# A gap of 288 bytes per partition in front of three large SBUF buffers

## The chip, the cores and the metric

The kernel runs on one core of a Trainium2 chip. The metric is the device time of one execution, in microseconds (us). Smaller is better.

## The reference, cut to what matters

The reference runs two small models one after the other on 256 tokens of width 1024: a block with multi-head latent attention, an mLSTM mixer and two squared-ReLU MLPs, then a block with a short convolution, a sparse attention with shared keys and values, and four SwiGLU feed-forward layers. Nearly all of its arithmetic is products of the token matrix with weights:

```python
D_MODEL = 1024; SEQ = 256; D_FF = 4 * D_MODEL; D_FF_2 = 2816

def sqrelu_mlp(h, w1, w2):
    return jnp.square(jax.nn.relu(h @ w1)) @ w2

def swiglu_ffn(x, w_in, w_out):
    gate, up = jnp.split(x @ w_in, 2, axis=-1)
    return (jax.nn.silu(gate) * up) @ w_out
...
y = mla_mixer(hn, ...)        # layer 0: projections 1024 to 384, 256, 32, back to 1024
y = mlstm_mixer(hn, ...)      # layer 1: projections 1024 to 3072, 8, back to 1024
x = x + y.astype(x.dtype)
x = x + sqrelu_mlp(rms_norm(x, norm_ffn[i]), ffn_w1[i], ffn_w2[i]).astype(x.dtype)
```

All of it is in float32, and each weight is used for all 256 tokens once.

## The kernel before, in words

**Split products.** A float32 product is made from three products in the type fp32r: a weight w is split into w_hi and w_lo, and a feature x into x_hi and x_lo, and w_hi·x_hi + w_hi·x_lo + w_lo·x_hi is added up in PSUM. All weights come from DRAM as a stream of 522 tiles `raw` of 128 partitions by 1024 floats (4096 bytes per partition). Each tile goes through a ring of four slots: SyncE issues the load, ScalarE makes `w_hi` from `raw` (line 510), VectorE makes `w_lo` as raw minus w_hi (line 968; GpSimd does 46 of the 522, line 448), and TensorE consumes it. Semaphores `tile_loaded`, `hi_ready`, `lo_ready` and `tile_done` tie the four together. A tile holds eight blocks of 128x128 weights, each 512 bytes per partition.

**The three forms of product.** TensorE's program (from line 1638 on) has:
- `product` (lines 1643 and 1644, in `residual`): a weight load of a w_hi block and one matmul of 512 columns, x_hi and x_lo together, out of `hs`; then a weight load of the w_lo block and a matmul of 256 columns, x_hi. It is used by down_0, down_1 and out_0 to out_3.
- `narrow_product` (lines 1651, 1652 and 1653, in `feature` and `residual_one`): three weight loads (w_hi, w_hi, w_lo), each with a matmul of 256 columns out of `xs`, `os` or `hs`. It is used by up_0, up_1, glu_0 to glu_3, cin and all the smaller projections.
- `token_major` (lines 1779 to 1781): the roles are turned. Blocks of 128 columns of `xs` or `os` are loaded as the weights, and the matmul streams 512 columns out of w_hi or w_lo. It is used by uk, uq, uv, mv, mo, kv and nq.

The attention's own products and its transposes (lines 1804 to 2034) are plain float32, with operands in `arena`, `kT`, `vtok` and `con`.

**The memory.** The helper `sb` allocates a tensor that stays for the whole kernel, one behind the other. First come raw, w_hi and w_lo (twelve buffers of 4096 bytes per partition), x, then many small ones, the last of them `vtok`, `kcT` and `vc`. Behind these lie three large regions. Two of them have two names each, since a tensor that is allocated and left at once gives its address to the next:

```python
        with nc.sbuf_tensor("os", [P, KD * 2 * S], F32R) as os_:
            pass
        bias = sb("bias", [P, H * S])
        with nc.sbuf_tensor("w1c_all", [P, 2 * 16 * P], F32) as w1c_all:
            pass
        xs = sb("xs", [P, KD * 2 * S], F32R)
        with nc.sbuf_tensor("hs", [P, FF1 * 2 * S], F32R) as hs:
            pass
        arena = sb("arena", [P, FF1 * 2 * S])
```

So `os` and `bias` are one region of 16,384 bytes, `w1c_all` and `xs` another of 16,384, and `hs` and `arena` a third of 65,536. Each chunk of x_hi or x_lo in `xs`, `os` and `hs` is 256 floats, 1024 bytes. All weight blocks begin at the same place modulo 512 bytes, and so do all chunks of xs, os and hs. Between the two places there are 32 bytes before the change: a chunk begins 32 bytes past a block modulo 512.

**The order of the work.** TensorE goes through the stages in the order of the network. Around the edited lines there are only allocations, no instruction. `bias` is filled once, by eight transfers that ScalarE issues before the sparse attention (line 939), when `os` is no longer in use.

```python
            def product(out_bank, lhs, k, src, first, last, hi=0):
                s, c = lhs
                chunk = k * 2 * S
                pe.matmul(bank(out_bank), w_hi[s][:, c:c + P], src[:, chunk:chunk + 2 * S], start=first, stop=False)
                return pe.matmul(bank(out_bank, 0, S), w_lo[s][:, c:c + P], src[:, chunk:chunk + S], start=False, stop=last)
...
                out = bank(out_bank, 0, S)
                pe.matmul(out, w_hi[s][:, c:c + P], x_hi, start=first, stop=False)
                pe.matmul(out, w_hi[s][:, c:c + P], x_lo, start=False, stop=False)
                return pe.matmul(out, w_lo[s][:, c:c + P], x_hi, start=False, stop=last)
```

Of the kernel before, what the change touches and what calls it, by code (L numbers as in the profile page):

```python
# [30 lines left out]
P = 128  # L31
# [105 lines left out]
def build(nc, x_in, tiles, vecs, rows, consts, rel_bias, w1c_k, w1c_v, w2c_k, w2c_v, y_out):  # L137
    ctx = ExitStack()
    with ctx:
        def sb(name, shape, dt=F32):  # L140
            return ctx.enter_context(nc.sbuf_tensor(name, shape, dt))
# [30 lines left out]
        kcT = sb("kcT", [P, G * NC])  # L172
        vc = sb("vc", [G * NC, G * DH])

        with nc.sbuf_tensor("os", [P, KD * 2 * S], F32R) as os_:
            pass
        bias = sb("bias", [P, H * S])
# [2031 lines left out]
```

## Time and profile before

| what | value |
|---|---|
| median of 3 runs | 1664.65 us (1664.22 to 1665.67) |
| the profiled execution's own time | 1666.71 us |
| its span, first to last instruction | 1664.9 us |
| mean granted clock of TensorE | 0.985 of full speed |
| TensorE matmul busy | 1602.7 us, 96% of the span |
| VectorE busy | 1099.6 us, 66% |
| ScalarE busy | 885.4 us, 53% |
| DMA | 282.81 MB, mean 170 GB/s |

A matmul's record begins when it starts and ends when its last result is modelled to be out, so records of successive matmuls overlap. The pace of TensorE is read from start to start, or from the number of matmuls in a stretch in which it never rests, and not from the duration of one.

### The profile page before, as it was taken

How to read it: one execution, taken by the hardware profiler on the slowest of the kernel's cores; microseconds unless marked ns; L12 is line 12 of the kernel's file. 1: busy time of each engine (PE TensorE's matmuls, PEld its weight loads, DVE VectorE, ACT ScalarE, POOL GpSimd, SP SyncE). 2: the span in 40 equal slices, each digit the busy share in tenths (PEclk: the TensorE clock that was granted, in tenths of full speed). 3: DMA queues.
4: the chain of work that ended last, by engine and by line, in shares of the span. 5: the costliest groups of instructions: out<-in, count | busy, mean ns of one | idle time of the engine just before them, and what ended most of it. 6: DMA issues, size and time to landing. Idle time of an engine off the chain costs nothing.

```text
span 1664.9 us, 33598 instructions
## 1 busy us (share of the span) xinstructions
PE 1602.7 (96%) x11652; PEld 1510.1 (91%) x11652; DVE 1099.6 (66%) x1770; ACT 885.4 (53%) x1468; POOL 163.7 (10%) x141
## 2 busy tenths in 40 slices
PE   7899999999999999999999999997999988799999
PEld 7789998977999899998999999897999867799997
DVE  6667766544876667667877666785566728676665
ACT  5676554535655445455446445544545546664443
POOL 1640000266000000000000000000000053300000
PEclk9999999989999999999999999998999989999999
DMA  6136566544566556556655555656455680055564
GB/s 228 64 82 199 188 190 190 176 131 135 178 190 188 191 176 198 182 187 203 191 188 189 190 188 187 206 182 196 145 189 186 210 171 15 1 175 186 184 197 142
DMA packets 81246, 282.81 MB, mean 170 GB/s; under 512 B 8848, under 2 KB 12432, under 8 KB 81168
## 3 DMA queue, kind: packets, MB, share of 16 engines
q1 hardware_dynamic: 77376, 276.88, 52.4%
q10 hardware_dynamic: 3792, 4.85, 1.7%
q8 instruction: 54, 0.88, 0.2%
q14 instruction: 24, 0.20, 0.0%
HBM read 280.12 MB, written 1.57 MB: 169 GB/s over the span
## 4 chain that ended last, share of the span: by engine, by line
PE 88%; DVE 5%; ACT 3%; issue 2%; DMA 1%; ACTq 1%; POOL 0%; DVEq 0%; SPq 0%; POOLq 0%
PE psum L1651 17%; PE psum L1653 17%; PE psum L1652 17%; PE psum L1643 17%; PE psum L1644 9%; PE psum L1779 2%; PE psum L1780 2%; PE psum L1781 2%; ACT arena L853 1%; DMA raw<-tiles 1%; DVE w_lo L968 1%; PE psum L2034 1%; PE psum L1941 1%; DVE arena L1517 0%; DVE arena L1516 0%
## 5 line engine op out<-in xcount | busy, mean ns | idle before, releaser
L510 ACT ACTIVATE w_hi<-raw 128x1024 fp32r<-128x1024 f32 x522 | 550.5, 1056 | 462.8 <-PE psum L1653 266.3
L968 DVE TENSOR_TENSOR w_lo<-raw,w_hi 128x1024 fp32r<-128x1024 f32 x476 | 582.0, 1223 | 229.0 <-ACT w_hi L510 228.2
L1651 PE MATMUL psum<-xs,w_hi 128*128 128x256 f32 x1960 | 550.7, 281 | 6.1 <-DVE w_lo L968 5.0
L1653 PE MATMUL psum<-xs,w_lo 128*128 128x256 f32 x1960 | 549.8, 280 | 0.0
L1652 PE MATMUL psum<-xs,w_hi 128*128 128x256 f32 x1960 | 547.9, 280 | 0.0
L1643 PE MATMUL psum<-hs,w_hi 128*128 128x512 f32 x1216 | 421.9, 390 | 0.0
L1651 PEld LDWEIGHTS psum<-xs,w_hi 128*128 128x128 f32 x1960 | 369.6, 189 | 7.2 <-DVE w_lo L968 5.5
L1652 PEld LDWEIGHTS psum<-xs,w_hi 128*128 128x128 f32 x1960 | 369.7, 189 | 0.2
L1653 PEld LDWEIGHTS psum<-xs,w_lo 128*128 128x128 f32 x1960 | 369.2, 188 | 0.0
L1644 PE MATMUL psum<-hs,w_lo 128*128 128x256 f32 x1216 | 343.4, 282 | 0.0
L1643 PEld LDWEIGHTS psum<-hs,w_hi 128*128 128x128 f32 x1216 | 228.3, 188 | 47.1
L448 POOL TENSOR_TENSOR w_lo<-raw,w_hi 128x1024 fp32r<-128x1024 f32 x46 | 110.3, 2411 | 1228.1 <-ACT w_hi L510 1198.0
L1644 PEld LDWEIGHTS psum<-hs,w_lo 128*128 128x128 f32 x1216 | 230.5, 190 | 0.0
L1651 PE MATMUL psum<-os,w_hi 128*128 128x256 f32 x544 | 154.5, 284 | 1.6 <-DVE os L1158 1.6
L1652 PE MATMUL psum<-os,w_hi 128*128 128x256 f32 x544 | 152.7, 281 | 0.0
L1653 PE MATMUL psum<-os,w_lo 128*128 128x256 f32 x544 | 152.6, 281 | 0.0
L1651 PEld LDWEIGHTS psum<-os,w_hi 128*128 128x128 f32 x544 | 103.2, 190 | 2.5 <-DVE os L1158 2.4
L1652 PEld LDWEIGHTS psum<-os,w_hi 128*128 128x128 f32 x544 | 103.2, 190 | 0.0
L1653 PEld LDWEIGHTS psum<-os,w_lo 128*128 128x128 f32 x544 | 103.1, 189 | 0.0
L991 DVE SCALAR_TENSOR_TENSOR xs<-x,vec,xs 128x256 fp32r<-128x256 f32 (+1 forms) x80 | 38.1, 482 | 51.7 <-ACT xs L524 51.7
L524 ACT ACTIVATE xs<-x,vec (+1 forms) x80 | 40.2, 509 | 54.3 <-DVE x L1058 31.2
L1106 DVE TENSOR_TENSOR fsum<-psum,sil 128x256 f32<-128x256 f32 x88 | 37.4, 425 | 46.0 <-PE psum L1653 44.7
(282 smaller groups left out, 1643.8 us busy)
## 6 DMA issues: line engine op xcount, KB each, us to landing
raw<-tiles SPq DMA_DIRECT2D x522, 512.0 KB, 4.2
bias<-bias_dram ACTq DMA_DIRECT2D x8, 256.0 KB, 12.5
x<-x_in SPq DMA_DIRECT2D x4, 256.0 KB, 5.7
y_out<-x SPq DMA_DIRECT2D x8, 128.0 KB, 3.5
con<-consts SPq DMA_DIRECT2D x1, 771.0 KB, 9.2
bias_dram<-bias_row ACTq DMA_DIRECT2D x1, 512.0 KB, 7.2
row<-rows SPq DMA_DIRECT2D x1, 192.0 KB, 9.2
vec<-vecs SPq DMA_DIRECT2D x1, 80.5 KB, 1.9
```

The lines of the kernel that those rows point to most:

```text
L448: pool.tensor_tensor(w_lo[s][:, :], raw[s][:, :], w_hi[s][:, :].bitcast(F32), ALU.subtract).then_inc(lo_ready, 1)
L510: act.activation(w_hi[s][:, :], raw[s][:, :], ACT.Copy).then_inc(hi_ready, 1)
L524: act.activation(dst, src, ACT.Copy, scale=gain).then_inc(xhi_ready, 1)
L968: dve.tensor_tensor(w_lo[s][:, :], raw[s][:, :], hi_of(w_hi[s][:, :]), ALU.subtract).then_inc(lo_ready, 1)
L991: dve.scalar_tensor_tensor(out=dst, in0=src, scalar=gain, in1=hi_of(hi), op0=ALU.mult, op1=ALU.subtract).then_inc(xs_ready, 1)
L1106: dve.tensor_tensor(f, bank(b, 0, S), sil[u // 2][:, :] if u % 2 else rb[:, :], ALU.mult).then_inc(out_read, 1)
L1643: pe.matmul(bank(out_bank), w_hi[s][:, c:c + P], src[:, chunk:chunk + 2 * S], start=first, stop=False)
L1644: return pe.matmul(bank(out_bank, 0, S), w_lo[s][:, c:c + P], src[:, chunk:chunk + S], start=False, stop=last)
L1651: pe.matmul(out, w_hi[s][:, c:c + P], x_hi, start=first, stop=False)
L1652: pe.matmul(out, w_hi[s][:, c:c + P], x_lo, start=False, stop=False)
L1653: return pe.matmul(out, w_lo[s][:, c:c + P], x_hi, start=False, stop=last)
L1779: pe.matmul(out, x_hi, w_hi[s][:, col:col + 512], start=c == 0, stop=False)
```

## The change

One allocation is added, of 72 floats (288 bytes) per partition, that nothing reads or writes. The three large regions behind it move up by 288 bytes, and so begin 320 bytes past the weight blocks modulo 512, where they began 32 past them. No instruction is added, removed or moved.

```diff
--- before.py
+++ after.py
@@ -172,6 +172,7 @@
         kcT = sb("kcT", [P, G * NC])
         vc = sb("vc", [G * NC, G * DH])
 
+        sb("apart", [P, 72])
         with nc.sbuf_tensor("os", [P, KD * 2 * S], F32R) as os_:
             pass
         bias = sb("bias", [P, H * S])
```

## Rows read from the trace of the kernel before

**Rows 1.** The page: its head, and the busy time of each engine.
```profile
span 1664.9 us, 33598 instructions
...
PE 1602.7 (96%) x11652; PEld 1510.1 (91%) x11652; DVE 1099.6 (66%) x1770; ACT 885.4 (53%) x1468; POOL 163.7 (10%) x141
```

**Rows 2.** The page: the chain that ended last, by engine and by line.
```profile
PE 88%; DVE 5%; ACT 3%; issue 2%; DMA 1%; ACTq 1%; POOL 0%; DVEq 0%; SPq 0%; POOLq 0%
PE psum L1651 17%; PE psum L1653 17%; PE psum L1652 17%; PE psum L1643 17%; PE psum L1644 9%; PE psum L1779 2%; PE psum L1780 2%; PE psum L1781 2%; ACT arena L853 1%; DMA raw<-tiles 1%; DVE w_lo L968 1%; PE psum L2034 1%; PE psum L1941 1%; DVE arena L1517 0%; DVE arena L1516 0%
```

**Rows 3.** Groups of instructions, shapes apart: xcount, busy us, mean ns, idle before.
```profile
L1651 PE MATMUL psum<-xs,w_hi 128*128 128x256 f32 x1960 | 550.7, 281 | 6.1 <-DVE w_lo L968 5.0 <-DVE xs L991 1.1
L1643 PE MATMUL psum<-hs,w_hi 128*128 128x512 f32 x1216 | 421.9, 390 | 0.0
L1644 PE MATMUL psum<-hs,w_lo 128*128 128x256 f32 x1216 | 343.4, 282 | 0.0
L1651 PE MATMUL psum<-os,w_hi 128*128 128x256 f32 x544 | 154.5, 284 | 1.6 <-DVE os L1158 1.6
L1779 PE MATMUL psum<-w_hi,xs 128*128 128x512 f32 x128 | 55.3, 432 | 0.2 <-DVE w_lo L968 0.2
L1779 PE MATMUL psum<-w_hi,os 128*128 128x512 f32 x34 | 14.3, 419 | 2.3 <-issue 2.3
L1651 PE MATMUL psum<-hs,w_hi 128*128 128x256 f32 x64 | 17.9, 280 | 0.0
```

**Rows 4.** Stretches: busy us and instructions per engine, clock, DMA share, GB/s.
```profile
420.00:520.00 100.00, 100.00 (x858) 99.95 (x857) 76.17 (x120) 62.25 (x112) 0.00 (x0) 1.00 0.61 186
640.00:720.00 80.00, 80.00 (x681) 80.00 (x681) 51.78 (x71) 38.25 (x56) 0.00 (x0) 1.00 0.59 188
```

**Rows 5.** Timeline of TensorE in down_0 (product): start us, duration us.
```profile
259.81 0.39 PE L1643 MATMUL psum<-hs,w_hi 128*128 128x512 f32 x1
260.04 0.28 PE L1644 MATMUL psum<-hs,w_lo 128*128 128x256 f32 x1
260.16 0.39 PE L1643 MATMUL psum<-hs,w_hi 128*128 128x512 f32 x1
...
262.12 0.28 PE L1644 MATMUL psum<-hs,w_lo 128*128 128x256 f32 x1
262.24 0.39 PE L1643 MATMUL psum<-hs,w_hi 128*128 128x512 f32 x1
```

**Rows 6.** Timeline of TensorE in mo (token_major): first and last of 40 starts.
```profile
372.36 0.40 PE L1781 MATMUL psum<-w_hi,xs 128*128 128x512 f32 x1
...
381.46 0.40 PE L1781 MATMUL psum<-w_hi,xs 128*128 128x512 f32 x1
```

**Rows 7.** Timeline of TensorE in the sparse attention, plain float32; x2 merges two.
```profile
1400.60 0.60 PE L2006 MATMUL psum<-kT,arena 128*128 128x256 f32 x2
1401.03 0.39 PE L2005 MATMUL psum<-kT,arena 128*128 128x128 f32 x2
1401.25 0.60 PE L2006 MATMUL psum<-kT,arena 128*128 128x256 f32 x2
1401.68 1.50 PE L2034 MATMUL psum<-vtok,arena 128*128 128x128 f32 x12
```

**Rows 8.** Groups on VectorE and ScalarE, moved buffers beside unmoved ones.
```profile
L1080 DVE TENSOR_TENSOR hs<-fsum,hs 128x256 f32 x144 | 60.4, 419 | 0.0
L1068 DVE TENSOR_TENSOR ssq<-ssq,sq 128x256 f32<-128x256 f32 x40 | 16.8, 420 | 0.0
L596 ACT ACTIVATE hs<-fsum 128x256 f32 x80 | 32.1, 401 | 1.1 <-DVE fsum L1106 1.1
L562 ACT ACTIVATE sq<-x 128x256 f32 x40 | 16.0, 401 | 0.0
```

**Rows 9.** The page, transfers: KB each, median us from issue to landing.
```profile
raw<-tiles SPq DMA_DIRECT2D x522, 512.0 KB, 4.2
bias<-bias_dram ACTq DMA_DIRECT2D x8, 256.0 KB, 12.5
```

**Rows 10.** Timeline of ScalarE's queue, and the chain that ended last: start us, us, what.
```profile
1331.38 0.35 ACTq L939 DMA_DIRECT2D bias<-bias_dram  x1
...
1342.19 12.90 DMA raw<-tiles
```

## The prediction

> **What bounds the kernel now.** I read the page first. TensorE is busy for 96% of the span and its weight loads for 91%, while VectorE stands at 66% and ScalarE at 53% [rows 1]. The chain that ended last confirms it: 88% of it is TensorE, and the eight lines of the three split products hold about 83 points of that [rows 2]. The groups by line tell how many matmuls that is, and that TensorE waited in front of the 1960 matmuls of line 1651 on xs for 6.1 us in all [rows 3]. So the time is the number of matmuls times the pace at which TensorE takes them, and the pace is the one thing that a shift of addresses could touch.
>
> The pace has to be read from start to start. In the stretch 420 to 520 us (narrow_product out of os, then xs) TensorE never rests at full clock and starts 858 matmuls in 100 us: **116.6 ns** each. In 640 to 720, the same code with xs in another layer, it is 80 us / 681 = 117.5 ns [rows 4]. In product, the starts of line 1643 at 259.81 and 262.24 us are seven pairs apart: 2.43 us / 7 = **347 ns** a pair; from each start of 1643 to that of 1644 it is 0.23 us (260.04 − 259.81), rounded to 10 ns, and the pair less a 256-column matmul of 117 gives 230 [rows 5]. In token_major, 39 intervals lie between 372.36 and 381.46 us: 9.10 / 39 = **233.3 ns** for 512 columns [rows 6].
>
> **What those paces hold that is not arithmetic.** At the level of 2.4 GHz, 256 columns at one a cycle are 106.7 ns and 512 are 213.3. The plain float32 products show how near TensorE comes to such a number with a weight load in front of each: two matmuls of 256 columns of line 2006 go from 1401.25 to 1401.68 us, 215 ns each, and the two of 128 columns of line 2005 from 1401.03 to 1401.25, 110 ns each [rows 7]. That is two cycles a column (213.3 and 106.7) and 2 to 3 ns on top. The split products have the same numbers of cycles and 10 ns (256 columns), 17 ns (the 512 of product) and 20 ns (the 512 of token_major) on top. So 7 to 18 ns per matmul are lost in the split products that are not lost in the plain ones. What takes them the trace does not name. It is not a fixed length: 512 columns cost 230 ns in product and 233.3 in token_major, with one weight load each. What differs there is which operand lies where: in product the stream begins 32 bytes past the weights modulo 512, in token_major it is the weights that lie 32 past the stream.
>
> **The change, part by part.** *Added instructions: none. Removed: none. Order: none.* The allocation is not written or read, so nothing waits for it. What it does is move os/bias, xs/w1c_all and hs/arena.
>
> *VectorE and ScalarE on the moved buffers: zero.* A 128x256 operation of VectorE takes 419 ns where it writes hs and 420 where it touches only unmoved buffers; on ScalarE it is 401 and 401 [rows 8]. If an address did cost them something, both have room: 76% and 62% busy in the densest stretch [rows 4].
>
> *Transfers: zero, between −2 and +2 us.* The 522 tiles go to raw, which does not move. The moved bias is filled by eight transfers of 12.5 us each, issued from 1331.38 us on [rows 9, 10], and here the DMA is not hidden: the chain waits 12.90 us for the tiles behind them, from 1342.19 on [rows 10]. The bytes stay the same, and no row shows that the place of a row modulo 512 costs a transfer anything; if it changed a sixth of that wait, it would be 2 us, which no side of the argument needs.
>
> *TensorE's plain products: zero to −0.5 us.* They are at 110 and 215 ns, and nothing can be won but the 2 to 3 ns.
>
> *TensorE's split products: the whole question.* There are 3 × (1960 + 544 + 64) = 7704 matmuls of narrow_product, 1216 pairs of product, and 3 × (128 + 34) = 486 matmuls of token_major [rows 3]. That makes 7704 + 2432 + 486 = 10,622 weight loads, each running beside a stream. No row shows a fp32r product at another offset than ±32, so the price is bounded. **Lower bound of the time:** every matmul falls to the pace of the plain ones: 7704 × (116.6 − 109) = 58.6, 1216 × (347 − 215 − 109) = 28.0, 486 × (233.3 − 215) = 8.9, in all −95.5 us. **Upper bound:** the nearest row for what an offset can do is the difference between 230 and 233.3, and read directly between starts (0.23) it is at most 5; I take 4.5 ns per load as the size of such an effect: 10,622 × 4.5 = +48 us. **What I take:** −4.5 ns per load, −48 us, which is also half of the lower bound. The reason for the sign: at 32 bytes' distance the two streams, which both move at 4 bytes a column through the same 512 residues, run close to each other; 320 sets them more than half a period apart. With the roles turned and the distance the other way the loss is larger, so the distance seems to matter, and the near one is the suspect. The loss also isn't a constant of the code: the same three lines go at 116.6 and at 117.5 ns in two layers [rows 4], as two streams would that fall into step in more than one way.
>
> The sum, for the profiled execution: 1666.71 − 48 = 1618.7 us. The median of the runs stands 2.06 us below that execution, so the forecast is 1664.65 − 48 = **1617 us**.
>
> *Is the next engine in the way?* In narrow_product a weight tile lasts 24 × 116.6 = 2.80 us; at 109 it would be 2.62. VectorE is busy 76.17 us in 100 there, 2.13 us per tile, ScalarE 1.74. A tile lands 4.2 us after issue [rows 9] and the ring holds four, 10.5 us at the faster pace. The DMA engines would rise from 0.61 to 0.65 busy [rows 4]. So nothing takes the gain back in the steady stages, and the stages in which TensorE waits for attention keep their time.
>
> **A rule against it.** TensorE's weight loads and streams do overlap here, and the loss beside them is 10 ns for 256 columns [rows 4]. The Trainium skill, TensorE: Matmul & The Clock Gate, section Step-by-step: what each phase is for, says that TensorE reads SBUF by two independent ports, one for the stream and one for LDWEIGHTS, so that loading weights takes no bandwidth from the running matmul; SBUF — State Buffer, section SBUF: two separate sides, adds that on the engines' side only the port pair shared by VectorE and GpSimd is contended. By that rule no address can matter and the time stays at 1664.65 us. The trace neither confirms nor refutes it: the plain products keep to it and the split ones lose something.
>
> **Rivals.**
> 1. *No change.* The 10 to 20 ns on top are the price of fp32r loads and streams as such, whatever their addresses; the 3 ns between product and token_major come from what stands before each matmul (a 256-column one in one, a 512-column one in the other). For it: plain products with operands at several offsets all keep their 110 and 215. Time: 1664.65, within 3 us. Chance 0.27.
> 2. *All of the loss goes.* 1664.65 − 95.5 = 1569. For it: the plain products prove that the pace can be had with a load per matmul. Against: the fp32r stream takes twice the bytes per cycle. Chance 0.10.
> 3. *Slower.* The streams pass each other at another point. If a load runs a fixed time behind the stream, or reads its columns in the other order, 320 can be the near distance and 32 the far one; then each load costs the 4.5 ns more: 1664.65 + 48 = 1712. It decides as soon as the pace of narrow_product is above 116.6; at the second level that the trace has, 117.5, it is 0.9 × 10,622 = +10 us, 1674. For it: the trace has no row at 320, and 32 may be good by luck. Chance 0.18.
> 4. *The gap does not do what it says*, because the allocator rounds or places it elsewhere. 288 is nine times 32, and all buffers behind it are allocated in order, so I see no way; what there is of it is in rival 1.
>
> **How the numbers follow.** The forecast, a partial gain of 15 to 75 us, has 0.45; its own range is 1590 to 1650. Together with rival 2, faster has 0.55, same (within 0.2%, 3.3 us, which is about what a measurement of this kernel can tell) 0.27, slower 0.18. The range has to take in the forecast, rival 1, most of the way to the floor and the small form of rival 3: 1580 to 1676. It leaves out about 0.07 below and 0.12 above.
>
> **What would show it.** Right: the stretch 420 to 520 us of the changed kernel holds over 870 matmuls (115 ns; 891 would be 112.2) with the same weight loads, the pairs of product come at less than 343 ns, token_major at less than 232, line 2006 stays at 215, and VectorE's 419 and 420 stay. The busy shares of VectorE and ScalarE rise slightly, as the same work lies in less time. Rival 1: 858 and 347 again. Rival 3: under 850. Wrong as a whole: the time moves though these paces don't, that is, by waits in attention or by the wait of 12.90 us behind the transfers of bias.

## The result, and the profile after

Over five runs the changed kernel takes 1674.46 us (1670.84 to 1676.04) where the kernel before takes 1665.67 us (1664.22 to 1666.79) beside it. The ratio is 1.0049, with a 95% interval of 1.0035 to 1.0064: **slower by half a per cent**. The profiled execution took 1674.46 us, with a span of 1672.7.

The page of the kernel after, its head and the busy time of each engine, against [rows 1]:

```profile
span 1672.7 us, 33598 instructions
...
PE 1613.2 (96%) x11652; PEld 1513.7 (90%) x11652; DVE 1100.1 (66%) x1770; ACT 885.8 (53%) x1468; POOL 163.9 (10%) x141
```

The same 33,598 instructions, and the same work on VectorE and ScalarE to within 0.5 us. Only TensorE is busy longer, by 10.5 us. All line numbers are one higher than before, because of the added line. The groups by line show which of TensorE's forms changed, against [rows 3] and [rows 8]:

```profile
L1644 PE MATMUL psum<-hs,w_hi 128*128 128x512 f32 x1216 | 427.2, 394 | 0.0
...
L1081 DVE TENSOR_TENSOR hs<-fsum,hs 128x256 f32 x144 | 60.4, 419 | 0.0
L597 ACT ACTIVATE hs<-fsum 128x256 f32 x80 | 32.2, 402 | 1.1 <-DVE fsum L1107 1.1
```

One 512-column matmul out of hs now shows 394 ns where it was 390. The means of narrow_product and of product's second matmul move by 3 ns at most, and downward. The durations say little, though; the pace says it. Stretches of the kernel after, TensorE alone (busy us and instructions, clock, DMA share, GB/s):

```profile
240.00:300.00 60.00, 60.00 (x341) 1.00 0.59 182
540.00:600.00 60.00, 60.00 (x346) 1.00 0.59 189
640.00:720.00 80.00, 80.00 (x681) 1.00 0.56 187
1210.00:1260.00 50.00, 50.00 (x444) 1.00 0.58 193
1490.00:1590.00 100.00, 100.00 (x851) 1.00 0.58 189
```

and the same stretches of the kernel before:

```profile
240.00:300.00 60.00, 60.00 (x348) 1.00 0.63 191
540.00:600.00 60.00, 60.00 (x348) 1.00 0.58 183
1210.00:1260.00 50.00, 50.00 (x431) 1.00 0.57 188
1490.00:1590.00 100.00, 100.00 (x859) 1.00 0.61 194
```

TensorE is never idle in any of them and its granted clock is 1.00, so the counts are paces. In down_0 (240 to 300 us) 341 matmuls instead of 348. In down_1 (540 to 600) 346 instead of 348, though it is the same code and the same buffer. In glu_3 (1490 to 1590) 851 instead of 859. In glu_0 (640 to 720) 681 in both [rows 4]. And in glu_2 (1210 to 1260) **444 instead of 431**: 112.6 ns a matmul, faster than anything in the trace before. The pairs of product in the kernel after:

```profile
259.72 0.40 PE L1644 MATMUL psum<-hs,w_hi 128*128 128x512 f32 x1
...
262.20 0.40 PE L1644 MATMUL psum<-hs,w_hi 128*128 128x512 f32 x1
...
539.67 0.39 PE L1644 MATMUL psum<-hs,w_hi 128*128 128x512 f32 x1
...
542.11 0.39 PE L1644 MATMUL psum<-hs,w_hi 128*128 128x512 f32 x1
```

Seven pairs each: 2.48 us / 7 = 354 ns in down_0 and 2.44 / 7 = 349 ns in down_1, where before it was 347 [rows 5]. The stretch that the prediction names for its test, up_1 with what stands before it, lies 5 us later in the kernel after:

```profile
425.00:525.00 100.00, 100.00 (x850) 1.00 0.56 184
```

That is 850 matmuls instead of 858. In token_major 40 intervals between 377.20 and 386.53 us are 233.3 ns each, as before. So the shift does change the pace of the split products. It changes it in steps, not everywhere alike, and mostly for the worse.

### The profile page after: what moved, and what is told of

Its sections match the earlier page's. It is cut to its first block, busy times and chain, and to the rows that moved or that the text cites. A ratio compares the mean times of both kernels' runs of the same rounds, so it can differ in the third digit from the quotient of the medians.

```text
span 1672.7 us, 33598 instructions
## 1 busy us (share of the span) xinstructions
PE 1613.2 (96%) x11652; PEld 1513.7 (90%) x11652; DVE 1100.1 (66%) x1770; ACT 885.8 (53%) x1468; POOL 163.9 (10%) x141
## 4 chain that ended last, share of the span: by engine, by line
PE 88%; DVE 5%; ACT 3%; issue 2%; DMA 1%; ACTq 1%; POOL 0%; DVEq 0%; SPq 0%; POOLq 0%
PE psum L1652 17%; PE psum L1654 17%; PE psum L1653 17%; PE psum L1644 17%; PE psum L1645 9%; PE psum L1780 2%; PE psum L1781 2%; PE psum L1782 2%; ACT arena L854 1%; DMA raw<-tiles 1%; DVE w_lo L969 1%; PE psum L2035 1%; PE psum L1942 0%; DVE arena L1518 0%; DVE arena L1517 0%
## 5 line engine op out<-in xcount | busy, mean ns | idle before, releaser
L511 ACT ACTIVATE w_hi<-raw 128x1024 fp32r<-128x1024 f32 x522 | 550.2, 1056 | 463.7 <-PE psum L1654 265.0
L969 DVE TENSOR_TENSOR w_lo<-raw,w_hi 128x1024 fp32r<-128x1024 f32 x476 | 582.1, 1223 | 229.8 <-ACT w_hi L511 228.9
L1644 PE MATMUL psum<-hs,w_hi 128*128 128x512 f32 x1216 | 427.2, 394 | 0.0
```

The costliest lines, as they stand in the source:

```text
L511: act.activation(w_hi[s][:, :], raw[s][:, :], ACT.Copy).then_inc(hi_ready, 1)
L969: dve.tensor_tensor(w_lo[s][:, :], raw[s][:, :], hi_of(w_hi[s][:, :]), ALU.subtract).then_inc(lo_ready, 1)
```

## The experiments

These theories stood at first. **A**: the distance between stream and weights sets the pace. **Its rivals**: the distance does not matter and something else in the kernel changed (B below), ScalarE and VectorE reading and writing beside TensorE set the paces (C), the absolute place of the streams counts, or only the mere presence of the gap. From part 4 on there is **A2**, a finer A: a distance allows several paces, and what ran just before a stage picks one. What is called distance below is how far the stream begins past its weights, in bytes.

**1. The products alone, at sixteen distances** (`e1_offsets_alone`). The core of the kernel, for each distance, with `m` in the place of xs and `w` in that of w_hi and w_lo:

```python
pe.matmul(bank(t % 4, 0, S), w[(t + (j == 2)) % 4][:, k * P:(k + 1) * P], m[:, 8 + k * 512 + (j == 1) * S:][:, 0:S], start=k == 0 and j == 0, stop=k == 7 and j == 2)
```

> This kernel computes nothing of the reference: it only runs the three forms of split product on filled buffers, at sixteen offsets of the streamed buffer against the weights (0 to 480 bytes in steps of 32), first with the other engines idle and then with ScalarE and VectorE copying 128x1024 tiles all the time. Theory A, the distance modulo 512 sets the pace: at 32 narrow_product goes at 116.6 ns and product at 347 ns a pair, at 320 at 117.7 and 351, and other offsets differ from both by ns. Theory B, the distance does not matter and the 351 came from something else in the kernel: all sixteen agree within 0.5 ns. Theory C, the paces come from ScalarE and VectorE reading and writing beside TensorE: the two passes differ.

The timeline of TensorE merges each group, so a pace is the step from one start to the next, divided by the number of matmuls. The rows are those of the distances 32, 64, 192 and 256, first narrow_product (x144), then product (x64, 32 pairs), and for 32 and 192 token_major (x48):

```profile
55.56 16.96 PE L91 MATMUL psum<-m,w 128*128 128x256 f32 x144
72.36 11.27 PE L95 MATMUL psum<-m,w 128*128 128x512 f32 x64
83.46 11.36 PE L98 MATMUL psum<-w,m 128*128 128x512 f32 x48
94.66 17.13 PE L102 MATMUL psum<-m,w 128*128 128x256 f32 x144
111.62 11.33 PE L106 MATMUL psum<-m,w 128*128 128x512 f32 x64
...
252.74 16.49 PE L146 MATMUL psum<-m,w 128*128 128x256 f32 x144
269.07 11.46 PE L150 MATMUL psum<-m,w 128*128 128x512 f32 x64
280.37 11.15 PE L153 MATMUL psum<-w,m 128*128 128x512 f32 x48
...
330.88 17.44 PE L168 MATMUL psum<-m,w 128*128 128x256 f32 x144
348.15 11.47 PE L172 MATMUL psum<-m,w 128*128 128x512 f32 x64
```

At 32, narrow_product goes at (72.36 − 55.56) / 144 = 116.7 ns and product at 11.10 / 32 = 346.9 ns a pair. At 64 narrow_product has 117.8, at 192 it has 113.4, and product 11.30 / 32 = 353.1. At 256 narrow_product has 119.9. All sixteen distances of the same trace, by their starts:

| distance | narrow_product, ns | product, ns a pair | token_major, ns |
|---|---|---|---|
| 32 and 288 | 116.7 | 347.0 | 233.3 |
| 64 and 320 | 117.8 | 348.8 | 233.4 |
| 96 and 352 | 119.9 | 350.3 | 234.0 |
| 128 and 384 | 120.0 | 350.9 | 232.2 |
| 160 and 416 | 118.7 | 347.0 | 233.2 |
| 192 and 448 | 113.4 | 353.1 | 228.9 |
| 224 and 480 | 118.3 | 352.8 | 233.2 |
| 256, and 0 in the second pass | 119.9 | 353.4 | 226.9 |

Three things follow. Theory A holds for the products by themselves, though the distance 320 gives 348.8 a pair and not the 351 that was expected. **The period is 256 bytes and not 512**: each pair of rows 256 apart agrees within 0.6 ns, so the change went from 32 to 64, the next step of 32, and not to the far side. And the second pass, with ScalarE and VectorE each busy 97% of the time, gave the same paces (narrow_product at 32, 116.7 again, at 192, 113.4 again), so theory C falls. GpSimd and the DMA queues rest in this run, so it says nothing of them.

**2. A gap of 512, a gap of 256, a gap in front of everything, a gap of 224** (`e2_gap512`, `e8_gap256`, `e3_front288`, `e4_gap224`). The edits are one line each:

```diff
-        sb("apart", [P, 72])
+        sb("apart", [P, 128])    # or 64, or 56; for e3 the 72 floats stand in front of raw
```

> A gap of 512 bytes instead of 288: the large buffers lie 32 bytes past the weights modulo 512 again, as before, at other addresses. Theory A (distance modulo 512): the time of before, 1665 us within 3 us, pairs of product at 347 ns. Rival (the absolute place, or the mere shift, or the build, costs something): 1670 to 1676 us as with the change.

> The gap of 288 bytes in front of all buffers: everything moves by 288, the distance between weights and streams stays 32. Theory A: 1665 us, pairs at 347 ns. Rival (the absolute address of the streams modulo 512 counts, not the distance): 1670 to 1676 us, pairs at 351 ns, as with the change.

> A gap of 224 bytes: the large buffers lie 256 past the weights modulo 512. Theory A: another time than at 32 and at 320, somewhere between 1655 and 1690 us, with the pace of the pairs that the offset 256 shows in the kernel with the products alone. Rival (only a whole multiple of 512 against anything else counts): 1670 to 1676 us like the change.

> A gap of 256 bytes, the large regions 288 past the weights. Period 256: the time of before, 1665 us within 3 us, pairs at 346.9 ns. Period 512: another time, as for the change (1672 us) or the gap of 224 (1694 us).

Measured, as ratios to the kernel before: gap 512, 1.0004 (0.999 to 1.0018); 288 in front of everything, 1.0000 (0.9988 to 1.0013); gap 256, 0.9996 (0.9985 to 1.0007); gap 224, **1.0175** (1.0153 to 1.0198), 1694.3 us. The gap as such costs nothing, moving everything together by 288 costs nothing, and the distances 32, 288 and 544 are one. The distance 256, which is 0 modulo the true period, is the slowest tried in the whole kernel, and 4 us outside the 1655 to 1690 that were expected for it. Its stretches in glu_0 and glu_3:

```profile
640.00:720.00 80.00, 80.00 (x669) 1.00 0.59 191
...
1490.00:1590.00 100.00, 100.00 (x834) 1.00 0.58 188
```

80 / 669 = 119.6 and 100 / 834 = 119.9 ns, as the products alone showed at 256.

**3. The weights moved instead of the stream, finer steps, and plain float32** (`e5_offsets_fine`).

> Again only products on filled buffers, nothing of the reference: distances 0 to 248 bytes in steps of 8, then pairs with the weights moved instead of the stream, then plain float32 products at distances 0 to 224. Theory A, the distance between stream and weights modulo 256 sets the pace: stream +32 with weights +32 gives what distance 0 gave (120 ns for narrow_product), weights +32 with the stream at 0 gives what 224 gave (118.3 ns), weights +32 and stream +64 what 32 gave (116.7), weights +64 and stream at 0 what 192 gave (113.4). Rival, the place of the stream alone counts: each pair gives what its stream's own place gave. Plain float32: no dependence, within 1 ns, as its stream takes half the bytes per cycle; the rival that any product depends on it would show some ns here too.

The timeline again. The groups are stream +32 with weights +32 (L416, L420), stream +224 (L424), stream +64 with weights +32 (L440, L444), weights +64 (L448), and plain float32 at the distances 0 and 32 (L463, L466, 64 matmuls each):

```profile
1279.53 17.43 PE L416 MATMUL psum<-m,w 128*128 128x256 f32 x144
1296.79 11.48 PE L420 MATMUL psum<-m,w 128*128 128x512 f32 x64
1308.11 17.20 PE L424 MATMUL psum<-m,w 128*128 128x256 f32 x144
...
1364.80 16.96 PE L440 MATMUL psum<-m,w 128*128 128x256 f32 x144
1381.60 11.26 PE L444 MATMUL psum<-m,w 128*128 128x512 f32 x64
1392.69 17.12 PE L448 MATMUL psum<-m,w 128*128 128x256 f32 x144
...
1448.59 13.97 PE L463 MATMUL psum<-m,w 128*128 128x256 f32 x64
1462.40 13.98 PE L466 MATMUL psum<-m,w 128*128 128x256 f32 x64
```

Both moved by 32 gives 17.26 us / 144 = 119.9 ns, what the distance 0 gives. Weights +32 alone gives 118.3, what 224 gives, in the same trace. Stream +64 with weights +32 gives 116.7 and, for product, 11.09 / 32 = 346.6, what 32 gives. It is the distance: moving the weights alone changes the pace as moving the stream alone does, and moving both does not. One pair misses: weights +64 gave 117.8 where the stream at 192 gave 113.4. Product agreed there (353.1 in both), so a narrow_product at one distance can go at two paces. The steps of 8 bytes in the same run add two things: product has its worst at 136, 360.0 ns a pair, and narrow_product is fast at one more place, 112, with 113.7. Plain float32 goes at 13.81 / 64 = 215.8 ns at all eight distances.

**4. Each part of the change alone** (`e9_hs_only`, `e10_os_xs_only`), and the change once more (`e12_change_again`). For e9 the gap of 72 floats stands in front of hs; for e10 it stands where the change has it and a second gap, `sb("apart_hs", [P, 56])`, brings hs back to 32 modulo 256.

> The gap of 288 bytes in front of hs alone: only product and the 192 matmuls of cout on hs see the distance of 64 modulo 256, xs and os stay at 32. Theory A: pairs of product at 349 or 353.6 ns (the change had both) instead of 346.9, 1216 of them, +2.6 to +8.1 us: 1668 to 1675 us, and narrow_product on xs as before. Rival, most of the change's loss comes from narrow_product on xs: within 2 us of before.

> os and xs 320 past the weights as with the change, hs brought back to 32 modulo 256 by a second gap of 224 bytes. Theory A: pairs back at 346.9 ns; narrow_product on xs at 117.8 instead of 117.0 ns, 5880 times, +4.7 us at most, less what os wins where it falls to 113: 1663 to 1671 us. Rival, the hs part is the smaller: 1670 us or more.

> The changed kernel again, for a second profile of the same program. Theory A2 (states that the entry into a stage decides): the pairs of product are at 349 or 353.6 ns in each stage but not in the same stages as the first time, and the stage glu_2 need not be at 113. Rival, each stage has its own fixed pace: stage by stage the same paces as in the first profile.

Ratios: hs alone 1.0042 (1.0025 to 1.0059), os and xs alone 1.0033 (1.002 to 1.0047), the change again 1.0068 (1.0047 to 1.0089). Times: 1671.98, 1671.40 and 1677.46 us, where the kernel before beside them took 1665.2. The stretches of down_0 and up_1 with only hs moved, then those of down_0, up_1 and glu_2 with only os and xs moved:

```profile
240.00:300.00 60.00, 60.00 (x341) 1.00 0.57 177
460.00:520.00 60.00, 60.00 (x517) 1.00 0.58 189
```

```profile
240.00:300.00 60.00, 60.00 (x348) 1.00 0.59 181
460.00:520.00 60.00, 60.00 (x512) 1.00 0.59 188
1210.00:1260.00 50.00, 50.00 (x427) 1.00 0.59 189
```

Each part slows just the form that reads the moved buffer: 341 in down_0 with hs moved, 512 and 427 in up_1 and glu_2 with os and xs moved, and what is not moved keeps its 348 or 517. Moving hs costs 6.8 us and moving os and xs 6.2. So each is about half of it, and e10 came out a little above the 1663 to 1671 that were expected of it. Together the two would be 13; the change has 8.8 and 12.3 in its two measurements. Two things that the whole change has and the parts have not make it cheaper. One is the fast glu_2: 444 matmuls in 50 us against 427, a pace that in this trace held for 912 of the stage's 1056 matmuls, from 1151 us on: 912 × (117.1 − 112.6) = 4.1 us. The other is product: with hs alone all six stages are at 353.3 ns a pair, while in the change down_1, out_0 and out_1, 608 pairs, are at 348.9, which is 608 × 4.4 = 2.7 us less. That leaves 13.0 − 6.8 = 6.2 us, where 8.8 were measured, and the intervals of these ratios are 2 to 3.5 us to each side. In the second profile of the change glu_2 was fast again (443 in 50 us), but down_1, at 346 in the first, came to 341:

```profile
540.00:600.00 60.00, 60.00 (x341) 1.00 0.59 186
```

So the same stage of the same program can run at more than one pace of its distance. It shows in the kernel before too: glu_0 holds 681 matmuls in 80 us there [rows 4], and 688 or 689 in the kernels of part 2 with the gaps 512, 256 and 288 in front, whose distance is the same. The expectation that all stages would be drawn anew was too strong: of the long stages only down_1 changed.

**5. The entry, the sizes, and bf16** (`e11_entries_and_sizes`, `e14_states_and_small_loads`).

> Products on filled buffers alone, nothing of the reference. First narrow_product and product at distances 32, 64 and 192, each after one matmul of 16 to 240 columns, so that the loads and streams meet at another phase. Theory A2, the pace locks into one of a few states and the entry decides which: at 64 product shows both 349 and 353 ns a pair, at 192 narrow_product both 113.4 and 117.8, while 32 keeps one. Rival, the distance alone decides: each distance shows one pace, whatever the entry. Then loads of 128, 64 and 32 columns under a stream of 256, and streams of 128, 384 and 512 under a load of 128: if the loss comes from the load's reads meeting the stream's, it falls with the columns of the load, from about 10 ns at 128 to about 3 at 32, and stays about the same for a longer stream; rival, it is a fixed toll of the fp32r stream: it grows with the stream and not with the load. Last bf16 at eight distances: with half the bytes, theory A expects 109 ns and no dependence, like plain float32.

> Products on filled buffers alone, nothing of the reference: sixteen distances in steps of 16 bytes, each entered in four ways, then loads of 128, 16, 4 and 1 column under streams of 256. Theory A2 (states, picked by the entry): at 64 and 192 narrow_product shows 113.3 and 117.8 ns, at 32 it shows 116.7 and 117.8, product keeps 346.6 at 32; whether one distance holds 113.3 for all entries is open. Then the small loads: if the meeting of the load's reads with the stream's is the loss, a load of one column leaves 109 to 110 ns at every distance; rival, the toll belongs to the stream and to the change from one matmul to the next: 113 to 117 ns remain with one column, with the distance still visible.

Groups of 96 matmuls of narrow_product, each behind one matmul of another length. At the distance 32 behind 48 and 144 columns (L82, L112), at 64 behind 16 and 48 (L152, L162). Then bf16 at 0 and 32, 64 matmuls of 256 columns each, all from the first of the two runs:

```profile
41.27 11.55 PE L82 MATMUL psum<-m,w 128*128 128x256 f32 x96
...
100.89 11.41 PE L112 MATMUL psum<-m,w 128*128 128x256 f32 x96
...
179.98 11.13 PE L152 MATMUL psum<-m,w 128*128 128x256 f32 x96
199.56 11.55 PE L162 MATMUL psum<-m,w 128*128 128x256 f32 x96
...
773.93 7.16 PE L400 MATMUL psum<-mb,wb 128*128 128x256 bf16 x64
780.92 7.15 PE L403 MATMUL psum<-mb,wb 128*128 128x256 bf16 x64
```

By starts within the groups, behind the first slow step of each, these are 117.8 and 116.7 ns at 32, 113.3 and 117.8 at 64, and in the same trace 113.3 and 117.8 at 192. Product held 346.6 at 32 for all eight entries, showed 348.9 and about 353.5 at 64, and 353.3 at 192 always. So a distance allows one pace or several, and what went before the stage picks one. It is not the one matmul alone. The second run has an entry of 16 columns at 64 as well, and there the group behind it (L232) goes at 117.8:

```profile
249.86 8.72 PE L232 MATMUL psum<-m,w 128*128 128x256 f32 x72
```

In fact all four entries at 64 gave 117.8 in this run, against what was expected. What differs is what ran ahead of the entry: product at the distance 32 in the first run and at 48 in the second. Which part of the history decides stays open. Nor are two paces the most: narrow_product at 160 had 117.4 and 120.0 here and 118.7 in part 1, and product at 48 had 346.8, 350.0 and 351.1. Of sixteen distances with four entries each, narrow_product reached 113.3 in all four only at **112**; product had 346.6 to 346.8 in all four at 16, 32, 144 and 160. bf16 goes at 6.99 / 64 = 109.2 ns at 0 and at 32, and at the other six distances too.

The first run also has streams of other lengths behind a full load. At the distance 0, 256, 384 and 512 columns go at 120.0, 173.3 and 226.7 ns, 13.3 above one column a cycle each time, which looks like a fixed toll. At 32 they go at 116.7, 176.7 and 233.3, which is 10, 17 and 20 above, so there it grows with the stream. Neither of the two expectations fits both.

The small loads contradict what was expected of theory A. Loads of 128, 16 and 1 column under a stream of 256, at the distance 0 (L710, L713, L719), then 128 and 1 at 32 (L722, L731):

```profile
937.98 7.82 PE L710 MATMUL psum<-m,w 128*128 128x256 f32 x64
945.64 7.42 PE L713 MATMUL psum<-m,w 128*16 128x256 f32 x64
...
960.15 7.42 PE L719 MATMUL psum<-m,w 128*1 128x256 f32 x64
967.40 7.64 PE L722 MATMUL psum<-m,w 128*128 128x256 f32 x64
...
989.82 7.63 PE L731 MATMUL psum<-m,w 128*1 128x256 f32 x64
```

At 0 a full load leaves 120.0 ns and a load of one column 113.3, so 6.7 ns of the loss go with the load's columns; in the first run they are gone already with a load of 64 columns (113.3). But 113.3 remain with one column, and at 32 it is 116.7 with either load. So at least 4 ns above bf16's 109.2 are left at every distance tried with the smallest load, and at 32 a load of one column costs what a full one does. A matmul behind a smaller load also writes fewer partitions of its result, and no run separates the two. How the stream's own loss, and its dependence on the place, comes about stays open.

**6. Better distances in the whole kernel** (`e6_gap160`, `e7_gap160_hs288`, `e15_os_xs_112`).

> A gap of 160 bytes, all three large regions 192 past the weights. By the paces of the products alone: narrow_product 113.4 instead of 116.9 ns, 7704 times, -27 us; product 353.1 instead of 346.9 a pair, 1216 times, +7.5 us; token_major 228.9 instead of 233.2, 486 times, -2.1 us: 1643 us. Rival, the paces in the kernel do not follow those of the products alone: within 5 us of 1665.

> os and xs 192 past the weights as in the last one, and hs, by a second gap of 96 bytes, 288 past, which is 32 modulo 256. Theory A with a period of 256: product keeps its 346.9 ns a pair, narrow_product on os and xs has 113.4, token_major 228.9: 1665 - 26.3 - 2.1 = 1637 us. Rival, only the modulus 512 of the description counts: the pairs of product are not at 346.9 and the time lies above 1640.

> os and xs 112 bytes past the weights modulo 256 (gaps of 64 and 256 bytes, and the streams begin 16 bytes into their buffers), hs at 32. With products alone, narrow_product showed 113.3 ns at 112 for each of four entries, product 346.6 a pair at 32. If the distance is the cause: narrow_product on os and xs 113.3 instead of 116.9 ns, 7512 times, -27 us, token_major as it was: 1638 us. Rival, in the kernel the tiles' waits and loop ends throw it into a slower state as they did at 192: 117 to 118 ns in the long loops and 1655 to 1668 us.

All three regions at 192: ratio 1.0007 (0.9992 to 1.0021), no gain. Its twelve executions fall into two groups, four from 1661.49 to 1665.5 us and eight from 1668.98 to 1672.28; the trace is of one of the eight, so what the quick ones did differently is not shown. With hs back at 32: 0.9967 (0.9953 to 0.9981), 1661.08 us beside 1666.54, so 5.5 us of the 28 expected. Both fail by the same thing: in the long loops narrow_product fell into the slower of the two paces that 192 allows (512 matmuls in 60 us in up_1 of the first, 117.2 ns), and only in shorter ones like cin into the faster (355 in 40 us, 112.7 ns). The one with 112 has this edit:

```diff
+        sb("apart", [P, 16])
-        with nc.sbuf_tensor("os", [P, KD * 2 * S], F32R) as os_:
-            pass
+        with nc.sbuf_tensor("os", [P, KD * 2 * S + 4], F32R) as os_room:
+            os_ = os_room[:, 4:4 + KD * 2 * S]
         bias = sb("bias", [P, H * S])
+        sb("apart_b", [P, 64])
...
-        xs = sb("xs", [P, KD * 2 * S], F32R)
+        xs_room = sb("xs", [P, KD * 2 * S + 48], F32R)
+        xs = xs_room[:, 4:4 + KD * 2 * S]
```

It takes **1645.52 us** (1641.51 to 1646.56) where the kernel before takes 1664.85 beside it: 0.9885 (0.9867 to 0.9904). Its stretches, with all engines:

```profile
460.00:520.00 60.00, 60.00 (x531) 60.00 (x531) 43.68 (x66) 36.16 (x68) 0.00 (x0) 1.00 0.61 193
640.00:720.00 80.00, 80.00 (x708) 80.00 (x708) 53.71 (x74) 40.29 (x60) 0.00 (x0) 1.00 0.59 194
...
240.00:300.00 60.00, 60.00 (x348) 53.18 (x347) 37.59 (x49) 27.47 (x38) 0.00 (x0) 1.00 0.58 186
```

60 / 531 and 80 / 708 are both 113.0 ns, in all long loops of the kernel alike, and down_0 keeps its 348. It is faster than the kernel before and the changed one. Of the 27 us expected it has 19.3 by the medians, while its profiled execution, the fastest of its four with 1641.51 us, is 25.2 below that of the kernel before. In that trace the paces are those expected; where the other three executions lose 4 to 5 us more is not shown.

## Why the prediction was wrong

The forecast was 1617 us and faster; measured were 1674.46 and slower. That lies within the range given, on the side to which 0.18 was given; the second measurement, 1677.46, lies just above the range.

*What held.* The kernel is bound by the pace of TensorE, and a shift of addresses moves that pace and nothing else: VectorE's rows of 419 and 420 ns came back as 419 and 419, ScalarE's as 402 and 401, two plain products of 256 columns of line 2007 go from 1405.83 to 1406.26 us in the kernel after, 215 ns each, and parts 2 and 4 leave nothing for other causes but what executions differ by. The chain's wait for the tiles behind bias was 14.59 us instead of 12.90, inside the 2 us that were set for it, and it was 10.7 to 14.0 in the kernels of parts 2 and 6 with gaps of other sizes, so the gap doesn't show in it.

*The step that failed* is "What I take" with its reason for the sign: "at 32 bytes' distance the two streams ... run close to each other; 320 sets them more than half a period apart". Two parts of it were wrong. The period: I took the 512 of the description for the period of the mechanism, and no row bore on it. The runs show 256, and 320 is 64, the neighbour of 32. And the rule that a greater distance is a faster one: the table of part 1 has no such order, with its best and its worst pace of product 32 bytes apart (347.0 at 32, 353.4 at 0), and with the best of narrow_product at 192, where product is among the slowest. The row that was taken as evidence of the sign, 233.3 ns in token_major against 230 in product, did not tell it either: token_major kept 233.3 at the distance 64. One price for all forms could not be right either, as each form has its own best distance.

*The size.* Instead of −4.5 ns on each of 10,622 loads, product became slower by 2.2 ns a pair in three stages and by 6.6 in the other three, which is 608 × 2.2 + 608 × 6.6 = +5.3 us. narrow_product went from 116.6 to 117.5 ns in up_1 and glu_3 and stayed at 117.5 in glu_0; with some 4,500 matmuls that lose 1.1 ns (the step from 116.7 to 117.8) and 912 in glu_2 that gain 3.4, it comes to +1.9 us. That estimate, +7.2 us in all, stands beside the 7.8 by which the profiled span grew.

*The rivals.* The third, slower, is what happened, in its small form: "at the second level that the trace has, 117.5, it is 0.9 × 10,622 = +10 us, 1674". That this number is the measured one to within 1 us is luck: it puts the same +0.9 ns on every load, and the runs show nothing on token_major, +2.2 to +6.6 on a pair of product, and a gain in glu_2. Its other reason, that 32 may be good by luck, is confirmed for product, whose 346.6 is the lowest seen at any distance (16, 144 and 160 share it). The first, no change, had the argument that plain products at several offsets all keep their pace. That was a fact about plain float32, which the runs show to be flat, and it said nothing of fp32r. The second was half right: 113.3 ns can be had, which is 3.3 to 4.2 ns less, but not 109, and only at another place; the run at 112 has −19.3 us.

*The row that could have told.* The two levels, 116.6 and 117.5 ns for the same code at the same distance [rows 4], were read as two ways of falling into step, and the entries of part 5 show that one distance does hold several paces. What I did not draw from it is that a new distance would bring its own set of such levels, and that nothing in the trace said whether the new set lies above or below.

*The rule of the Trainium skill.* TensorE: Matmul & The Clock Gate, section Step-by-step: what each phase is for, has loads and streams on two independent ports, so that a load takes nothing from a running matmul. For bf16 the runs agree: 109.2 ns at each of eight distances. For plain float32 they agree as far as the distance goes (215.8 at each). For fp32r they do not: the pace of a 256-column matmul runs from 113.3 to 120.0 ns with the place of the weights against the stream, whichever of the two is moved, and at the distance 0 a load of 128 columns leaves the stream 6.7 ns slower than one of 16. The measurement decides. What in the reading of the two makes it so, no run here shows.

## What to carry to other kernels

Where TensorE is bound by fp32r products with a weight load in front of each, the place of the streamed buffer against the weights, modulo 256 bytes, is worth one or two per cent: here from −1.2% (os and xs at 112, hs at 32) to +1.8% (all at 256). Sweep it in a kernel of nothing but the products, each form by itself, with several entries for each distance, because one distance can hold several paces. Here the distances that showed one pace for every entry (112 and 0 for narrow_product, 32 for product) kept it in the whole kernel, and at 192, which showed two, the long loops took the slower. Count matmuls in stretches without idle time to read it; durations of single matmuls hardly show it.

## What the runs showed of the hardware that was not expected

- The pace of fp32r products repeats every 256 bytes of the distance between stream and weights; a move of both together changes nothing (119.9 ns at 0, by either way).
- Within a stage the pace is steady, and the same values return at many distances: 113.3, 116.7, 117.8 and 120.0 ns for matmuls of 256 columns, with others between them at some distances (117.1 at 240, 118.3 at 48, 119.3 at 176). Three of the four are 272, 280 and 288 cycles of 2.4 GHz, 8 apart.
- Which level of a distance is taken depends on what ran before the stage: at 64, 113.3 behind one matmul of 16 columns and 117.8 behind one of 48, for all that follow in the group. The same 16 columns gave 117.8 where something else ran ahead of them.
- The loss does not need the load's columns: with loads of one column 113.3 ns remain at 0, 64, 96, 128 and 192, and 116.7 at 32, against 109.2 in bf16.
- ScalarE and VectorE, both busy 97% of the time beside TensorE, changed none of the paces of part 1.
